# Gate and up projections with the weights stationary and the tokens moving

## The reference, cut to what matters

```
def swiglu(x, w_gate, w_up, w_down):
    return (jax.nn.silu(x @ w_gate) * (x @ w_up)) @ w_down
```

## Time and profile before

| | us |
|---|---|
| median of three runs | 2744.25 |
| lowest, highest | 2743.05, 2745.86 |
| span of the profiled execution | 2740.7 |
| PE busy | 2693.0 |
| DVE busy | 1550.6 |
| ACT busy | 1219.4 |

### The profile page before, as it was taken

The page is one execution under the profiler, slowest core; times in us unless marked ns, Lnnn a source line. Parts: engine busy times, 40 slices in busy tenths (PEclk is TensorE's granted clock), DMA queues, the critical chain, the costliest instruction groups (busy, mean ns, idle before and its releaser), DMA issues.

```text
span 2740.7 us, 36529 instructions
## 1 busy us (share of the span) xinstructions
PE 2693.0 (98%) x12832; PEld 2244.7 (82%) x12832; DVE 1550.6 (57%) x1766; ACT 1219.4 (44%) x1488; POOL 128.9 (5%) x164
## 2 busy tenths in 40 slices
PE   9999999999999999999999999999999999999996
PEld 7888888888777888888888888888788888888885
DVE  5445444455566665577777765445664454445555
ACT  4444443433344443465565554443344444443333
POOL 1000000000000000122211100000000000000000
PEclk9999999999999999999999999999999999999998
DMA  7556565666654545655665555667656555657663
GB/s 233 185 183 197 179 198 185 222 195 194 187 163 139 145 145 181 205 176 182 180 181 175 176 180 169 195 192 240 195 191 197 185 184 184 199 188 255 223 192 122
DMA packets 285635, 513.76 MB, mean 187 GB/s; under 512 B 19616, under 2 KB 52560, under 8 KB 282992
## 3 DMA queue, kind: packets, MB, share of 16 engines
q1 hardware_dynamic: 279616, 485.03, 57.3%
q0 software_dynamic: 4336, 25.36, 2.5%
q10 hardware_dynamic: 1600, 2.26, 0.2%
HBM read 506.23 MB, written 6.36 MB: 187 GB/s over the span
## 4 chain that ended last, share of the span: by engine, by line
PE 97%; DVE 1%; DMA 1%; ACT 0%; issue 0%; POOL 0%; SPq 0%; ACTq 0%; POOLq 0%; DVEq 0%
PE acc L673 31%; PE acc L675 30%; PE acc L674 30%; PE spare L642 3%; PE spare L902 1%; DVE w_lo L1311 0%; PE spare L796 0%; PE spare L795 0%; DMA seg<-acs_rows 0%; PE spare L789 0%; PE spare L909 0%; PE spare L894 0%; PE spare L771 0%; PE spare L770 0%; DMA resid<-x 0%; ACT w_hi L1000 0%
## 5 line engine op out<-in xcount | busy, mean ns | idle before, releaser
L1311 DVE TENSOR_TENSOR w_lo<-land,w_hi 128x1024 fp32r<-128x1024 f32 (+2 forms) x960 | 1154.2, 1216 | 998.0 <-ACT w_hi L1000 991.8
L1000 ACT ACTIVATE w_hi<-land 128x1024 fp32r<-128x1024 f32 (+2 forms) x960 | 971.2, 1024 | 1016.1 <-PE acc L675 948.4
L673 PE MATMUL acc<-w_hi,a_hi 128*128 128x512 f32 (+1 forms) x2592 | 1002.3, 387 | 5.1 <-DVE w_lo L1311 4.4
L675 PE MATMUL acc<-w_hi,a_lo 128*128 128x512 f32 (+1 forms) x2592 | 984.1, 380 | 0.0
L674 PE MATMUL acc<-w_lo,a_hi 128*128 128x512 f32 (+1 forms) x2592 | 982.2, 379 | 0.0
L673 PEld LDWEIGHTS acc<-w_hi,a_hi 128*128 128x128 f32 x2592 | 488.4, 188 | 102.2 <-issue 10.4
L675 PEld LDWEIGHTS acc<-w_hi,a_lo 128*128 128x128 f32 x2592 | 487.9, 188 | 93.6
L674 PEld LDWEIGHTS acc<-w_lo,a_hi 128*128 128x128 f32 x2592 | 488.7, 189 | 91.4 <-issue 3.6
L673 PE MATMUL acc<-w_hi,g_hi 128*128 128x512 f32 x704 | 274.0, 389 | 0.0
L675 PE MATMUL acc<-w_hi,g_lo 128*128 128x512 f32 x704 | 273.9, 389 | 0.0
L674 PE MATMUL acc<-w_lo,g_hi 128*128 128x512 f32 x704 | 273.9, 389 | 0.0
(11 more groups left out here) (223 smaller groups left out, 1483.1 us busy)
## 6 DMA issues: line engine op xcount, KB each, us to landing
land<-w_in SPq DMA_DIRECT2D x232, 512.0 KB, 3.9
land<-ffn_w_gate SPq DMA_DIRECT2D x176, 512.0 KB, 4.4
land<-ffn_w_up SPq DMA_DIRECT2D x176, 512.0 KB, 4.5
land<-ffn_w_down SPq DMA_DIRECT2D x176, 512.0 KB, 4.4
land<-w_ssd_o SPq DMA_DIRECT2D x64, 512.0 KB, 4.1
land<-w_attn_o SPq DMA_DIRECT2D x32, 512.0 KB, 4.3
land<-w_in SPq DMA_DIRECT2D x128, 128.0 KB, 2.3
land<-w_out SPq DMA_DIRECT2D x32, 512.0 KB, 4.5
```

The lines of the kernel that those rows point to most:

```text
L673: pe.matmul(to, rows_hi, hi, start=first, stop=False)
L675: mm = pe.matmul(to, rows_lo, hi, start=False, stop=last)
L1000: act.activation(w_hi[:, l % SPLIT, :, 0:width], land[:, l % LAND, :, 0:width], ACT.Copy).then_inc(high, 1)
L1311: dve.tensor_tensor(w_lo[:, l % SPLIT, :, 0:width], land[:, l % LAND, :, 0:width], w_hi[:, l % SPLIT, :, 0:width].bitcast(F32), ALU.subtra ...
```

## The change

The gate and up projections swap their operands. `slab_across` takes a 128 x 128 block of the weights as the stationary operand and all 256 tokens as the moving one. A slab is 2 row blocks x 4 column blocks x 3 products, which makes 24 matmuls with 256 moving columns. The result stands channel-major in `acc`: two column blocks share a bank of 512. SiLU and product are as before, on tiles of the same size, and `prod` is now already in the layout of `g_hi` and `g_lo`. `up_turn` and its bank waits are gone. ACT copies `prod` to `g_hi` in one instruction of 128 x 1024 (`hidden_high`, before slab 4; in the down projection before slab 5), DVE writes `g_lo` in one (`hidden_rest`, before slab 5; in the down projection before slab 6). Two new semaphores order them, `g_high` and `g_out`; PE waits for `g_out` in the down projection before slabs 0 and 20, and POOL before it loads the residual stream.

```
+            def slab_across(phase, i, l):
+                pair, use = acc_use(phase, i, l // 8)
+                s = l % 8
+                if s == 0 and not (isinstance(use, int) and use == 0):
+                    pe.wait_ge(acc_out[pair], use)
+                pe.wait_ge(rest, slab_no(phase, i, l) + 1)
+                for k in range(2):
+                    for c in range(TPG):
+                        to = acc[:, 2 * pair + c // 2, (c % 2) * SEQ:(c % 2 + 1) * SEQ]
+                        hi, lo = (w[:, l % SPLIT, k, c * P:(c + 1) * P] for w in (w_hi, w_lo))
+                        first, last = s == 0 and k == 0 and c % 2 == 0, s == 7 and k == 1 and c % 2 == 1
+                        pe.matmul(to, hi, a_hi[:, 2 * s + k, :], start=first, stop=False)
+                        pe.matmul(to, hi, a_lo[:, 2 * s + k, :], start=False, stop=False)
+                        mm = pe.matmul(to, lo, a_hi[:, 2 * s + k, :], start=False, stop=last)
+                mm.then_inc(used, 1)
...
-                    if not first and l == 4:
-                        up_turn(phase, i - 1)
-                    slab(phase, i, l // 8, l % 8, a_hi, a_lo)
+                    slab_across(phase, i, l)
...
-                        if j == 0 and l == 2:
-                            up_turn(phase, NC_F - 1)
-                        if j == 0 and l == 20:
-                            wait_bank(phase, NC_F - 1, "ga")
-                            wait_bank(phase, NC_F - 1, "gb")
+                        if j == 0 and l in (0, 20):
+                            pe.wait_ge(g_out, hidden_no(phase, NC_F - 1 + l // 20))
...
-                    if not first and l == 6:
-                        high_tiles(phase, i - 1, ("ga", "gb"), g_hi, (i - 1) * 4)
+                    if not first and l == 4:
+                        hidden_high(phase, i - 1)
...
+            def hidden_high(phase, i):
+                pair, use = acc_use(phase, i, 1)
+                act.wait_ge(acc_out[pair], use + 1)
+                act.activation(hidden_tiles(g_hi, i), prod, ACT.Copy).then_inc(g_high, 1)
...
-                if not (isinstance(i, int) and i == 0):
-                    bank_ready(phase, i - 1, "gb")
                 dve.tensor_tensor(prod, silu_t, upper_half, ALU.mult).then_inc(acc_out[pair], 1)
+            def hidden_rest(phase, i):
+                dve.wait_ge(g_high, hidden_no(phase, i) + 1)
+                dve.tensor_tensor(hidden_tiles(g_lo, i), prod, hidden_tiles(g_hi, i).bitcast(F32), ALU.subtract
+                                  ).then_inc(g_out, 1)
...
-                    if not first and l == 7:
-                        rest_tiles(phase, i - 1, ("ga", "gb"), g_hi, g_lo, (i - 1) * 4)
+                    if not first and l == 5:
+                        hidden_rest(phase, i - 1)
...
 (POOL, hidden_complete)
-                bank, use = spare_use(phase, NC_F - 1, "gb")
-                pool.wait_ge(bank_in[bank], use + 1)
+                pool.wait_ge(g_out, hidden_no(phase, NC_F))
```

More of the change, by code:

```diff
@@ L98 @@
     "xT": (1, LN_USES),
-    "up1": (NC_F, [("ga", 0), ("gb", 1)]),
     "ln1": (1, LN_USES),
@@ L107 @@
     "ln2": (1, LN_USES),
-    "up2": (NC_F, [("ga", 0), ("gb", 1)]),
 }
-SPLIT_USES = {"xT": LN_USES, "up1": SPARE["up1"][1], "ln1": LN_USES, "attn": [("oa", 2), ("ob", 3)],
-              "ssd": [("ya", 2), ("yb", 3)], "merge": SPARE["merge"][1], "ln2": LN_USES, "up2": SPARE["up2"][1]}
+SPLIT_USES = {"xT": LN_USES, "ln1": LN_USES, "attn": [("oa", 2), ("ob", 3)],
+              "ssd": [("ya", 2), ("yb", 3)], "merge": SPARE["merge"][1], "ln2": LN_USES}
 DEC_V = 4
@@ L169, in spare_use, with hidden_no @@
         at += n * per
+def hidden_no(phase, i):
+    return i if phase == "up1" else NC_F + i
 def high_no(phase, u, what):
@@ L253, in build_decoder_layer, with hidden_tiles @@
         prod = resid[:, :, W:2 * W]
+        def hidden_tiles(g, i):
+            return g[:, bass.ds(i * 4, 4), :].rearrange("p (a k) n -> p a (k n)", a=2)
         at0 = -(-nc.sbuf_base // 32) * 32
@@ L339, in build_decoder_layer @@
         tile_hi = sem("tile_hi")
+        g_high = sem("g_high")
+        g_out = sem("g_out")
         v_seq = sem("v_seq")
@@ L1076, in ffn @@
                     for l in range(44):
-                        if j == 0 and l == 6:
-                            high_tiles(phase, NC_F - 1, ("ga", "gb"), g_hi, (NC_F - 1) * 4)
+                        if j == 0 and l == 5:
+                            hidden_high(phase, NC_F - 1)
                         split(f"down{f}", j, l)
@@ L1437, in down @@
                             product(f"up{f}", NC_F - 1)
-                        if j == 0 and l == 7:
-                            rest_tiles(f"up{f}", NC_F - 1, ("ga", "gb"), g_hi, g_lo, (NC_F - 1) * 4)
+                        if j == 0 and l == 6:
+                            hidden_rest(f"up{f}", NC_F - 1)
                         if l in (18, 36):
```

## The result

The changed kernel takes 2780.59 us (median of 4 runs, 2780.22 to 2781.19) against 2744.72 us (4 runs) for the kernel before: 1.0132 times as long, 95% interval 1.012 to 1.0143. That is 36 us slower; 2780.8 us was forecast. The profiled execution has a span of 2779.6 us.

The account below looks back on a forecast made before the run. PE's own stream was taken to bound the kernel, busy 98% of the span. Span 2740.7 plus 36.7 us gave 2777.4; 3.55 us from span to median gave 2780.9, stated as 2780.8 us, range 2768 to 2791.

Parts of the forecast that it names:

- The pace of the narrow matmul: Up projections: 256-wide matmuls start 0.1200 us apart, as in existing rows of that form; 384 make 46.08 us a unit.
- Rival 1: Up projections: the fixed part belongs to moving weights, so moving activations run near the load's 0.107 us; 2671 us; 5%.
- the 13.3 ns: Fixed part of each matmul on PE beside its streaming, claimed equal at 512 and 256 moving columns.
- The transposes: Eight per unit on PE's path, claimed to cost 0.89 us a unit; the change removes them.
- The sum: 22 units in PE's stream, each going from 44.41 to 46.08 us: +36.7 us in all.
- 3.55 us: Whole kernel: the median of the runs was taken to lie this far above the profiled span.
- The hand-over: `prod` to `g_hi` and `g_lo` at unit ends: costed at nothing, at most 1.2 us a unit, 26 us in all.
- POOL's load: Residual stream load, now after `g_lo` at about 514.7 instead of 508.60; lands by 526 with 17 us of slack.
- PE's waits: PE's time waiting for DVE's `w_lo`, 7.9 us in all before, was to grow no larger.
- Rival 2: Up projections: the load's 13 ns cover breaks or instructions come late; each 10 ns a matmul costs 84 us, 2865 us; 4%.

Follow-up runs that it names:

- e1: Kernel before with the 512-wide moving weights of the gate and up projections cut into two of 256, activations stationary, transposes kept: 2799.0 us, ratio 1.0198.
- e9: Kernel before; first up projection: 256-wide moving weights, mostly 64-token stationary blocks; second: moving operands of 384 and 128 columns, full loads: 2875.66 us.
- e4: Kernel after with stationary blocks of 64 weight columns instead of 128, except in each group's first and last row block: 2731.17 us.
- e2: Kernel after with the old 512-wide slab and no transposes, leaving the transposition out of the computation: 2720.45 us, ratio 0.9915 to the kernel before.
- e6: Old 512-wide slabs, hidden layer transposed by DVE in 32 x 32 blocks and moved by ACT, nothing left out: 2724.16 us, 0.9928 of the kernel before.
- e5: Kernel after with the 256 tokens cut into two moving operands of 128, each with its own full weight load: 5376.6 us.
- e8: As e5, with stationary blocks of 64 columns except in the first and last row block of each group: 2890.72 us.
- e3: Kernel after with the three products reordered so no two consecutive matmuls within a block share a stationary block: 2780.39 us.

## Why the prediction was right

**The pace of the narrow matmul**, 0.1200 us from the B and C slabs, held in the changed kernel over 8448 matmuls, in unbroken streams of thousands. Taking the price from rows of the same form, rather than from half of the wide one, was what decided: half of 0.2267 would be 0.1133 us, 43.5 us a unit, and would have given a gain of 20 us. **Rival 1** (moving weights carry the fixed part) fell with the changed kernel's own 0.1200 us, and e1 and e9 confirm it: the pace doesn't depend on the roles. The Trainium skill, "TensorE: Matmul & The Clock Gate", section "Back-to-back issue gap", gives the rule of N/2.4 plus 2.5 ns for an isolated matmul, and says that at small N it has no budget for the weight load. The prediction left that condition out. The changed kernel's 0.1200 us stand 11 ns above the rule's 109.

**What the 13.3 ns are** the prediction had only in part. It said that they belong to the matmul whatever its width. That holds for full blocks at 256 and 512 columns; with half blocks e4 shows 6.7 ns. The forecast didn't need more, since all its blocks are full.

**The transposes** were sized at 0.89 us and on the path; e2 says 0.90.

**The sum**, +36.7 us, stands beside +35.9 for the medians and +38.9 for the spans. That the forecast of the time came within 0.2 us is luck. It added 3.55 us to go from the span to the median. In the runs that list both, a run's time is only 1.6 to 1.9 us above its own span, 1.6 in the profiled run of the kernel after (2781.19 against 2779.6). By that the profiled execution of the kernel before, whose own time isn't listed, took about 2742.3 us, less than any of its four runs. The 2 us that this term had too much made up for 2.2 us that the sum had too little. The spans differ from the sum by 2.2 us, at a place the prediction didn't name: the first slabs of the state-space stage. Rows of the kernel before, then of the kernel after, timeline of PE:

```profile
1123.64 0.50 PE L673 MATMUL acc<-w_hi,a_hi 128*128 128x512 f32 x1 [2.41 <-DVE w_lo L1311]
```

```profile
1142.58 0.50 PE L680 MATMUL acc<-w_hi,a_hi 128*128 128x512 f32 x1 [3.30 <-DVE w_lo L1331]
...
1144.25 0.63 PE L680 MATMUL acc<-w_hi,a_hi 128*128 128x512 f32 x1
1144.68 0.63 PE L681 MATMUL acc<-w_lo,a_hi 128*128 128x512 f32 x1
1145.10 0.63 PE L682 MATMUL acc<-w_hi,a_lo 128*128 128x512 f32 x1
```

Busy time by stretch there, kernel after (sum, PE busy, PEclk, DMA share, GB/s):

```profile
1143.00:1148.00 5.00, 5.00 (x17) 0.66 0.91 302
1148.00:1153.00 5.00, 5.00 (x24) 1.00 0.52 139
```

The wait is 0.9 us longer, and a little behind it the matmuls are 0.43 us apart: the clock was at its low level for 3.4 us, which costs 1.6 us. The profiled execution of the kernel before has no such fall there; whether its other runs have it isn't on record. The new roles aren't needed for it: e1 has the same fall, behind 3.05 us between the starts. Between the starts at this place lie 2.79 us in the kernel before and 1.94 us in e2, with no fall; in e6 it is 3.33 us, with a fall. That is 3.0 of e6's 3.7 us behind e2 (1.4 of gap and 1.6 of clock). Why the wait varies from kernel to kernel was not followed up; the code there is the same in all.

**The hand-over** cost nothing, as worked out. Timeline of ACT in the kernel after, around unit 0's end:

```profile
60.58 1.06 ACT L1014 ACTIVATE w_hi<-land 128x1024 fp32r<-128x1024 f32 x1 [1.88 <-PE acc L699]
61.88 1.06 ACT L1088 ACTIVATE g_hi<-resid 128x1024 f32 x1 [0.25 <-DVE resid L1428]
63.40 1.06 ACT L1014 ACTIVATE w_hi<-land 128x1024 fp32r<-128x1024 f32 x1 [0.45 <-PE acc L699]
```

ACT waits 0.25 us for the product and is then still 0.45 us early for slab 4, which waits for PE. POOL's load was expected to leave at 514.7 on the old time axis; it leaves 9.2 us behind the last product's start, where 12.6 was allowed (rows of the kernel after):

```profile
530.59 0.73 POOL L542 DMA_DIRECT2D resid<-x  x1 [520.15 <-DVE g_lo L1433]
...
resid<-x POOLq DMA_DIRECT2D x1, 2048.0 KB, 11.0
```

PE's waits didn't grow in the up projections: waits for `w_lo` were 7.9 us in all and are 8.3 now, and the place just named alone has 0.9 more:

```profile
PE acc L680 <- DVE w_lo L1331: 8.3, 8, 3.3
```

**Rival 2**, the thin cover of the load, didn't strike, but e5 shows how near it is: one halving of the moving operand further, the load sets the pace, the clock stays at its low level, and the kernel takes twice as long. The prediction priced this edge at 0.227 us a matmul by adding load and stream; in e5 they don't add, and a load at half the clock sets the pace.

## What to carry to other kernels

A matmul with a full load has a price beside its moving columns at 2.4 GHz, so of two layouts with the same work and full loads the one with the wider moving operand won here: count matmuls and loads, not only columns, and take the price from the rows of the same form. A transposition that is saved is worth its time on PE, here 0.9 us for eight; the layout that saves it cost 2.56 us for 192 more matmuls. When PE bounds and DVE and ACT are half idle, take the transposition off PE and leave the wide matmuls alone.

## What the runs showed of the hardware

- With full loads and 128 moving columns PE stayed at 1.2 GHz for the whole second up projection, though the profile shows it busy 100% of the time: 0.213 us a matmul (e5). With half loads, the same width and the same number of matmuls it stayed at 2.4 GHz, 0.060 us (e8). Busy PE in the profile doesn't mean full clock. PEclk tells the clock, but only from where its record begins: for e5's first up projection it read 1.00, at the same 0.213 us and with 512-wide matmuls 0.43 us apart right behind it.
- At 2.4 GHz the fixed part of an fp32r matmul is 13.3 ns at 256 and 512 moving columns with a block of 128 columns, and 6.7 ns at 128 and 256 with one of 64. At 512 the smaller block made it slower, 0.2300 against 0.2267 us, and nothing here explains it.
- At 1.2 GHz full loads left nothing beside the stream: 0.213 us for 256 columns and 0.427 for 512 (kernel after, where PEclk reads 0.50).
- A repeated stationary block is not cheaper (e3).
- DVE's transposition of 32 x 32 blocks took 0.69 us for 128 x 512 values, and ACT's copy between groups of 32 partitions 0.41 us for 32 x 256.
